# Identity products in TensorE's waits, in a two-block transformer kernel on one core

## The reference

```python
# block 1, per layer: three mixers side by side, then MLP, then a gated embedding
y = rms_norm(x, in_g) @ w_in + b_in
m = mlstm(...)                    # 4 heads of 64, chunks of 64, exponential gates
h = hgrn2(...)                    # 4 heads of 64, chunks of 32, decays by exp of sums
s = window_attention(...)         # 8 query heads, 2 key heads, window 128, sinks
x = x + concat(m, h, s) @ w_out
x = x + square(relu(rms_norm(x) @ w_up)) @ w_down
x = x + sigmoid(rms_norm(x) @ w_ple_gate) * rms_norm(p @ w_ple_proj)
# block 2, per layer: attention (dilated in layer 0, differential in layer 1),
# cross-attention over 256 memory rows, SwiGLU; each with a norm before and after
h = h + rms_norm(attention(rms_norm(h)), g)
h = h + rms_norm(cross_attention(rms_norm(h), mem), g)
h = h + rms_norm(swiglu(rms_norm(h)), g)
```

## Time and profile before

| | us |
|---|---|
| median of three runs | 3154.83 |
| lowest and highest | 3149.82, 3155.75 |
| the profiled execution | 3154.28 |
| its span in the trace | 3152.5 |

### The profile page before, as it was taken

The page is one execution under the profiler, slowest core; times in us unless marked ns, Lnnn a source line. Parts: engine busy times, 40 slices in busy tenths (PEclk is TensorE's granted clock), DMA queues, the critical chain, the costliest instruction groups (busy, mean ns, idle before and its releaser), DMA issues.

```text
span 3152.5 us, 37380 instructions
## 1 busy us (share of the span) xinstructions
PE 3034.2 (96%) x14772; PEld 2398.3 (76%) x14772; DVE 1782.2 (57%) x2507; ACT 1258.8 (40%) x2021; POOL 304.9 (10%) x236
## 2 busy tenths in 40 slices
PE   7999999999999999999998999999999989999998
PEld 5677888887767888886667877888766678778886
DVE  7765644457765644467675535344567756353444
ACT  6645432245644332344445433232434445332222
POOL 2011100011011100011001112000200011020001
PEclk9999999999999999999999999999999999999999
DMA  3111323222111223222112322232211123223232
GB/s 137 54 48 49 97 96 98 96 94 86 54 42 62 96 94 100 94 97 75 56 54 93 108 73 81 94 101 94 80 61 54 47 87 114 70 77 100 94 100 80
DMA packets 73721, 259.07 MB, mean 82 GB/s; under 512 B 8020, under 2 KB 10200, under 8 KB 73176
## 3 DMA queue, kind: packets, MB, share of 16 engines
q1 hardware_dynamic: 72824, 252.99, 24.7%
q0 software_dynamic: 736, 3.87, 0.3%
HBM read 254.73 MB, written 2.10 MB: 81 GB/s over the span
## 4 chain that ended last, share of the span: by engine, by line
PE 80%; DVE 8%; issue 7%; ACT 2%; DVEq 1%; POOLq 1%; DMA 0%; POOL 0%; ACTq 0%
PE bank L490 67%; DVE w_lo L1990 2%; PE bank L1004 1%; PE bank L679 1%; POOLq L2808 1%; PE bank L1015 1%; PE bank L1210 1%; PE bank L1189 1%; PE bank L959 1%; PE bank L1025 1%; ACT w_hi L1313 1%; PE bank L1029 1%; DVE der L2528 1%; PE bank L709 0%; PE bank L721 0%
## 5 line engine op out<-in xcount | busy, mean ns | idle before, releaser
L490 PE MATMUL bank<-a_hi,w_hi 128*128 128x512 f32 x2168 | 874.3, 403 | 39.8 <-DVE w_lo L1990 16.0
L490 PE MATMUL bank<-a_hi,w_lo 128*128 128x512 f32 x2168 | 852.9, 393 | 0.0
L490 PE MATMUL bank<-a_lo,w_hi 128*128 128x512 f32 x2168 | 852.7, 393 | 0.0
L1990 DVE TENSOR_TENSOR w_lo<-w_raw,w_hi 128x1024 fp32r<-128x1024 f32 (+1 forms) x474 | 607.5, 1282 | 289.8 <-ACT w_hi L1313 288.2
L1313 ACT ACTIVATE w_hi<-w_raw 128x1024 fp32r<-128x1024 f32 (+1 forms) x474 | 494.7, 1045 | 409.5 <-DMA w_raw<-weights 409.0
L490 PE MATMUL bank<-b_hi,w_hi 128*128 128x512 f32 (+1 forms) x1560 | 590.9, 379 | 8.4 <-DVE w_lo L1990 4.9
L490 PE MATMUL bank<-b_lo,w_hi 128*128 128x512 f32 (+1 forms) x1560 | 582.7, 374 | 0.0
L490 PE MATMUL bank<-b_hi,w_lo 128*128 128x512 f32 (+1 forms) x1560 | 582.5, 373 | 0.0
L490 PEld LDWEIGHTS bank<-a_hi,w_hi 128*128 128x128 f32 x2168 | 412.8, 190 | 149.6 <-issue 40.9
L490 PEld LDWEIGHTS bank<-a_hi,w_lo 128*128 128x128 f32 x2168 | 412.1, 190 | 88.7
L490 PEld LDWEIGHTS bank<-a_lo,w_hi 128*128 128x128 f32 x2168 | 412.8, 190 | 85.8 <-issue 3.8
(11 more groups left out here) (306 smaller groups left out, 2878.5 us busy)
## 6 DMA issues: line engine op xcount, KB each, us to landing
w_raw<-weights SPq DMA_DIRECT2D x458, 512.0 KB, 3.4
w_raw<-weights SPq DMA_DIRECT2D x16, 384.0 KB, 2.9
x<-x SPq DMA_DIRECT2D x8, 256.0 KB, 7.7
mem<-mem POOLq DMA_DIRECT2D x2, 1024.0 KB, 5.2
out<-x SPq DMA_DIRECT2D x8, 256.0 KB, 2.1
mem<-mem SPq DMA_DIRECT2D x1, 1024.0 KB, 12.5
ple<-ple POOLq DMA_DIRECT2D x2, 512.0 KB, 3.9
o<-c_level SPq DMA_DIRECT2D x1, 512.0 KB
```

The source lines that it names most:

```text
L490: last = mm(bank[unit_bank(u) if at is None else at][:, 0:cols], w[:, u % SLOTS, ks], t[:, k, 0:cols], start=(k == begun and n == 0), stop ...
L1990: tt(w_lo[:, u % SLOTS, w], w_raw[:, u % SLOTS, w], f32(w_hi[:, u % SLOTS, w]), ALU.subtract).then_inc(w_lo_ready, 1)
```

## The change

A new helper on TensorE, `kept_busy(b, n, cols)`, multiplies the identity (128 x 128) by the first `cols` columns of a constant tile into a PSUM bank that nobody reads at that point, n times. It is called at 19 places of the code, 105 products of 512 columns and 16 of 256 in all: around the column sums (1, 2 and 8; without the 2 and 8 in the last layer), ahead of `prepare` (1) and of the third level's scores (4), in eight window steps (256 columns), ahead of the first (2) and the fifth tile (4) of the output product, in round 1 (6) and round 8 of block 2's attention and behind it, and in `kv` (4). Where the bank could still be read, a wait comes ahead of it. Two further edits take blocks of small products apart: the half units behind `prepare` and behind the second `gates` become two quarters (six dense products) between the four-row products, and the five tiles' sums of squares (`norm_sums`) become two, two and one, with the level scores and a half, and then a half, between them; two tiles' sums in the window steps are taken apart over two steps. The other engines' programs stay as they are.

```diff
+            def kept_busy(b, n, cols=S):
+                for _ in range(n):
+                    mm(bank[b][:, 0:cols], ident, small[:, 0:cols], start=True, stop=True)
...
-            def y_columns():
+            def y_columns(followed=True):
                 pe.wait_ge(sq_added, c.count(sq_added, 7))
                 pe.wait_ge(root_ready, c.groups)
                 column_sums(SUM_BANK, sq_sum, True, False)
+                kept_busy(7, 1)
                 pe.wait_ge(y_squared, c.count(y_squared))
                 column_sums(SUM_BANK, y[:, 18, :], False, True)
+                if followed:
+                    kept_busy(7, 2)
                 spread_root(SUM_BANK)
+                if followed:
+                    kept_busy(7, 8)
...
+                def quarters():
+                    u, h = c.unit, turn_of["half"]
+                    if h == 0:
+                        pe.wait_ge(w_lo_ready, u + 1)
+                        pe.wait_ge(bank_free, u - 1)
+                    for k in range(4 * h, 4 * h + 4):
+                        last = products(u, k, a, 8, S, at=bank_in(first, u))
+                        if k == 4 * h + 1:
+                            yield
...
+                def busy_in_next(n):
+                    pe.wait_ge(bank_free, c.unit - 1)
+                    kept_busy(bank_in(first, c.unit), n)
...
-                    gates(0)
+                    quarter = quarters()
+                    gates(0, quarter)
                     pe.wait_ge(g_end, l + 1)
                     for p in range(2):
                         last = mm(bank[6 + p][:, :], heads_c[0:4, qs(p)], m_row[0:4, 3, :], start=True, stop=True)
+                        if p == 0:
+                            next(quarter)
...
-                def gates(p):
+                def gates(p, quarter):
                     if p:
                         pe.wait_ge(m_w_made, 2 * (8 * l + 4))
                     for e in range(2):
+                        if e:
+                            next(quarter)
...
-                def norm_sums(tiles, done):
+                def norm_sums(tiles, done, at=0, ended=True):
                     pe.wait_ge(g_sq, done)
-                    for j, t in enumerate(tiles):
+                    for j, t in enumerate(tiles, at):
...
-                    last.then_inc(g_nsum, 1)
+                    if ended:
+                        last.then_inc(g_nsum, 1)
...
                 halves_of(4)
+                busy_in_next(1)
                 prepare()
-                half()
...
                 sums(3)
-                gates(1)
-                half()
+                quarter = quarters()
+                gates(1, quarter)
+                next(quarter)
                 scores(4)
...
                 halves_of(2)
+                busy_in_next(4)
                 level_scores(2)
...
-                norm_sums(G_SQ_QK, 9 * l + 7)
+                norm_sums(G_SQ_QK[0:2], 9 * l + 4, 0, False)
                 level_scores(7)
-                halves_of(2)
+                half()
+                norm_sums(G_SQ_QK[2:4], 9 * l + 6, 2, False)
+                half()
+                norm_sums(G_SQ_QK[4:5], 9 * l + 7, 4)
...
                 for s in range(16):
+                    if s in (2, 3, 4, 5, 6, 7, 11, 12):
+                        pe.wait_ge(a_copied, 16 * l + s - 1)
+                        if s == 11:
+                            pe.wait_ge(a_kept, 4 * l + 2)
+                        kept_busy(4 + s % 2, 1, 2 * P)
...
                     if s == 13:
+                        pe.wait_ge(a_copied, 16 * l + 13)
+                        kept_busy(4, 2)
                         out_begun(OUT_ORDER[0:1])
...
-                out_begun(OUT_ORDER[3:8])
+                out_begun(OUT_ORDER[3:4])
+                pe.wait_ge(a_kept, 4 * l + 3)
+                kept_busy(4, 4)
+                out_begun(OUT_ORDER[4:8])
...
+                    if r == 1:
+                        kept_busy(F_O, 6)
                     score(r - 1, 0)
...
                     if more:
                         half(0)
+                    else:
+                        kept_busy(W_BANK[0] if diff else F_R, 3)
                     score(r - 1, 2)
...
                     elif diff:
+                        pe.wait_ge(f_copied, turns(l, PAIRS) - 2)
+                        kept_busy(F_T[1], 3)
                         norm_spread(4)
                         norm_spread(5)
+                        kept_busy(F_T[1], 1)
...
                 for _ in range(2):
                     unit(h, cols=MEM)
+                kept_busy(7, 4)
                 with c.loop(3, {}, 4):
...
-                y_columns()
+                y_columns(l + 1 < LAYERS)
```

16 lines of the change are left out of this document (15 added, 1 removed).

## The result

The change made the kernel slightly slower. Its median is 3158.03 us over 22 executions, that of the kernel before, timed beside it, 3151.78 over 22: a ratio of 1.0021, 95% interval [1.0015, 1.0028], so about 6 us slower where 4.4 us faster was forecast. The profiled execution has a span of 3157.4 us.

The account below looks back on a forecast made before the run. The prediction took TensorE (busy 3034 of 3152.5 us) as the bound. About 37 us returned by the clock against about 32 us paid made -4.4 us, from 3154.8 to some 3150 us; range 3138 to 3161.

Parts of the forecast that it names:

- three column sums: Column sums followed by a layer: added products make later work late, the clock returns little; together +1.8 us.
- gate rows: Block 1, both gate places: quarters between four-row products keep the clock up; net -5.0 us over both layers.
- level scores: Third level's scores: four products outlast their slot by 0.6 us, 1.75 us of clock loss returns; twice, -2.3 us.
- sums of squares: Column sums between halves: taken apart, they avoid a 1.7 us clock loss but bare the root, 1.2 us; -1.0 us.
- window and output: Window steps win 2.4 us; products at step 13 and ahead of the fifth output tile cost 4.2 us; sum +1.8 us.
- block 2 in all: Round 1, last rounds, key and value: products outlasting waits nearly balance the returned clock; sum +0.3 us.
- The bare copies: Gate rows, layer 0: the half unit no longer covers ScalarE's copy of the last row; 1.0 us lost.
- The returned clock: Whole kernel: about 37 us returned, mean clock 0.99 or more, stretches at 0.50 from 19 to a few.
- Rival 3: Whole kernel: identity products don't count for the clock, nothing returns, 32 us are paid; 3187 us, chance 0.05.
- The late products: Whole kernel: products outlasting their waits are paid in full; with waits laid bare, about 32 us.
- Rival 2: Block 1: other engines set the pace, so 10.7 us won vanish while late products are paid; 3160.6 us, chance 0.18.
- Rival 1: Last rounds and window steps: slack absorbs lateness, about 10 of 32 us go unpaid; 3140 us, chance 0.25.

Follow-up runs that it names:

- all_but_gates: The changed kernel with block 1's gate rows (prepare, second gates and their one product) written as before: 3155.08 us, ratio to the kernel before 1.0006.
- moves_only: The changed kernel without any of the 121 identity products; quarters, split sums and window waits stay: 3155.24 us, ratio to the kernel before 1.0006.
- y_only: The kernel before plus only the identity products around the column sums of y (1, 2, 8): ratio to the kernel before 1.0009.
- ends_covered: The changed kernel with prepare's second quarter moved behind both end-row products: 3153.74 us, ratio to the kernel before 1.0004.
- half_of_products: The changed kernel with 72 identity products instead of 121: 3140.06 us, ratio to the kernel before 0.9960.
- quarter_of_products: The changed kernel with 43 identity products instead of 121: 3143.64 us, ratio to the kernel before 0.9976.

## Why the prediction was wrong

The direction was wrong, and the cause is the price. Place by place, over the profiles of all kernels (mean of the changed form minus mean of the old form, us; n is the number of stretches measured in the old and in the new form):

```
place                          forecast  measured   old    new    n
three column sums                +1.8     +1.6
gate rows: prepare, each layer   -1.05    +2.4     23.14  25.50  20, 10
gate rows: second, each layer    -1.45    -0.45    24.94  24.49  20, 16
level scores, each layer         -1.15    -0.35    20.80  20.44  16, 12
sums of squares, each layer      -0.5     -0.3     26.83  26.52  16, 20
window and output, each layer    +0.9     +0.15    70.76  70.91  14, 8
block 2 in all                   +0.3     +2.6
sum                              -4.4     +7.0     (timed: +6)
```

The means rest on few profiles: where a low stretch comes and goes, one stretch differs from the next by up to 4 us, so a tenth in the table is not to be trusted.

**The failed step** is the gate rows: "With quarters of dense work between the rows I expect the clock to stay up: 1.5 us from the rows and 1.9 us from the half unit. Against this: ... the half unit no longer covers ScalarE's copy of the last row." Forecast -5.0 us, measured +3.8 by place and +3 to +4.7 by `all_but_gates`: 8 to 10 of the 10 to 11 us by which the forecast missed. Three things went into it:

- The clock did not stay up in layer 0 (71.2 to 81.4 us at 0.50). Prepare took 27.40 us there, against 24.19 in the profile of before and 22.97 in `moves_only`, at full clock: +3.2 us where -2.2 was forecast.
- Splitting has a price of its own, which I had put at nothing. In layer 0 the place of the second gate rows takes 23.90 us in the old form where the clock stays up there (in `y_only`), and 24.30 us with the quarters. And prepare in layer 1 is at full clock in the changed kernel, as was hoped, and takes 23.26 us; before it took 22.16, with 3.4 us at 0.50 in it. `moves_only` takes 22.42, so the identity product costs 0.84 us (in the forecast 0.87 less a wait of 0.1). With 1.18 us for the bare copies that leaves 0.9 us returned where I had counted 1.65; the missing 0.7 fits the two splits there.
- The second gate rows did win 1.1 us in either layer in the pair of profiles (forecast 1.45), but the old form had no low stretch there in 9 of 20 stretches, and so the mean is 0.45.

The bare copies were in the sum and nearly right: 1.0 us forecast, 1.18 us measured, in either layer. `ends_covered` covers them and wins 4.3 us, but in its profile mostly because the low stretch is shorter.

**The returned clock** was right in sum: 37 forecast, 35 measured, 0.98 to 0.995, 19 stretches to three. The other signs came as well: the waits for a_lo behind the column sums are gone from TensorE's list, and the pair behind the one shown starts 2.7 us later. Rival 3, that the products don't count, is refuted. The rule of the Trainium skill, page TensorE: Matmul & The Clock Gate, in the part on PE-mode transpose, that a transpose in that mode doesn't count as busy in the same way, doesn't reach products issued as ordinary matmuls with the identity: with them the clock is 0.995, and 0.983 in `moves_only`.

**But the return was priced from one profile.** In block 2, layer 0, I counted low stretches of the one trace as if each execution had them. Over nine profiles with the old form there, the last round takes 48.05 us on average and not the 49.21 of that trace, and key and value 12.59, not 13.42. The changed form takes 50.06 and 13.03 each time. So +0.4 and about -0.4 became +2.0 and +0.4. The level scores are the same: 21.53 us in that trace, 20.80 on average, as some traces have no low stretch there (19.6 to 20.1). The unchanged kernel's own executions have clocks from 0.977 to 0.983. The same page of the Trainium skill says, in the section What's actually happening, that the number of slow matmuls at a kernel's start varies between runs of one kernel; this case has the like in the middle of a kernel, and I should have given the returns a discount for it.

**The late products** were sized well where I worked them out from a row: the three column sums +1.2, +0.2 and +0.4 against +1.2, +0.2 and +0.35 in the pair of profiles (+1.6 in sum over all), root bare for 1.2 us against 1.20, round 1 of layer 0 +1.8 against +1.9 in the pair (+1.5 over all). The output's products were not timed apart from the window steps.

**Rival 2** (other engines pace block 1) had a time of 3160.6 us, 5.8 above before, and the measured 6 us fit it. Its mechanism isn't what happened. The sign that I had named for it did show: from the first unit product behind the second gates to the first of these level scores it took 38.9 us before (103.52 to 142.44) and 39.6 after (105.11 to 144.67), not less. But that stretch was at full clock before, so a steady clock had nothing to win in it, and the four products outlast the wait; the sign was badly chosen. What decides is whether the time won ahead of the wait for h_d was lost in it. It wasn't: from ahead of the second gates to behind the level scores the same unit products took 67.3 us before and 65.0 after. **Rival 1** asked whether lateness is absorbed; it isn't, each superfluous product cost 0.35 us.

**What the forecast didn't ask** is whether so many products are needed. It took the counts as given. The first 72 cost about 15 us and return 29 (from `moves_only` to `half_of_products`), the other 49 cost 17 and return nothing.

Open: why the clock falls in prepare in one kernel and not in another with the same code there (22.97 us without, 27.40 with the one product; 24.84 in `half_of_products`). I tried no kernel that shifts only the time at which it is reached. Open also is how far the 0.39 us for each us holds in single places; it is a mean over the kernel. Which of the 49 products were the ones that cost most I didn't time one by one.

## What to carry to other kernels

A filler in a wait has to be shorter than the wait: put in the fewest products, read what is left of the wait in the trace, and stop while something is left; here 72 products held the clock as well as 121, and the difference was 17 of 3158 us; 43 held it less well. Splitting dense work to put it between small products isn't free: it cost 0.4 us a place at full clock here, and where the work covered a signal's way to another engine and back, that way lay bare as well (1.18 us). And price a clock's return from several executions (time against clock), never from the stretches of a single trace.

## What the runs showed that I had not expected

- A wait left open doesn't always bring the clock down: ahead of the level scores it fell in 10 of 16 stretches with 2.4 to 2.7 us open, and in none of 8 with one or two products, of which one left 1.87 us open in layer 0 of `quarter_of_products`.
- The time hangs on the clock within one and the same kernel, with 0.39 us for each us at 0.50; over the 22 executions of the changed kernel, 3153.3 us came with clock 0.997 and 3163.5 with 0.993.
- Dense quarters between four-row products didn't decide the clock: prepare with the same quarters had 0, 3.4 or 10.2 us at 0.50, depending on the kernel around it.
